# GpSimd subtracts a quarter of each weight piece of the second block, VectorE three quarters

## The chip, the cores and the metric

The kernel is written in Bass, engine by engine, with semaphores between the engines, and runs on one core of one Trainium2 chip. The metric is the device time of one execution in microseconds (us), the median of several runs. A profile of one execution is read with it. Its engines are PE (TensorE matmuls), PEld (its weight loads), DVE (VectorE), ACT (ScalarE), POOL (GpSimd) and SP (SyncE, which here issues the DMAs).

## The reference, cut to what matters

Two transformer stacks run one after the other on 256 tokens of width 1024. The first (`first_block`) has a hybrid mixer, an MLA mixer and two expert layers. The change is in the second, which has two equal layers:

```python
h = x
for i in range(DEPTH):                      # DEPTH = 2
    hn = rmsnorm_2(h, ln_mix[i])
    (aq, ak, av, hy, gq, gk, gv, go, glr, gates) = split_cols(hn @ w_in[i], IN_SPLITS)
    y_a = attention_mixer(aq, ak, av, attn_qnorm[i], attn_knorm[i], cos, sin) @ w_br_attn[i]
    y_b = hyena_mixer(hy, hy_conv[i], spec, hy_skip[i]) @ w_br_hyena[i]
    y_c = gla_mixer(gq, gk, gv, go, glr, gla_w_lr[i], gla_b_lr[i], gla_onorm[i]) @ w_br_gla[i]
    mixed = gate[:, :, 0] * y_a + gate[:, :, 1] * y_b + gate[:, :, 2] * y_c
    h = h + mixed @ w_out[i]
    h = h + memory_cross_attention(rmsnorm_2(h, ln_x[i]), rmsnorm_2(mem, ln_mem[i]), ...)
    hn = rmsnorm_2(h, ln_mlp[i])
    h = h + jnp.square(jax.nn.relu(hn @ mlp_w1[i])) @ mlp_w2[i]
```

All of it is float32. Every `@` with a weight matrix is such a product as the change touches.

## The kernel before, in words

**Products in three passes.** A float32 product is made of float32r products, whose operands keep fewer bits. Each weight piece `w` is split into a high part (ACT copies it to float32r) and a low part (`w` minus the high part, float32r again), and so is each activation. PE then adds up high x high, high x low and low x high (L374, L375, L376 in `split_steps`; L434 to L436 where tokens are the output rows; L404 and L406 in `paired_steps`, the last product of the MLP, with the first two passes in one matmul of 512 columns; L2020 to L2022 in `three_passes`).

**Pieces.** Weights come by DMA into the three slots of a ring in `big`, 4096 columns each. A slot is two pieces of 2048 columns (8 chunks of 256, 4 of 512 or 16 of 128). The high part goes to one of two places, `hot_split` and `high_split` in turn; the low part is written over the weights themselves (`ring_split` is `big` by another name). For piece p:

- ACT, `split_high` (L465): waits for the DMA and until PE is done with piece p-2, whose place it takes, copies, and raises `w_high`.
- DVE, `split_low` (L473): waits for `w_high`, subtracts, and raises `w_split`.
- PE, `next_piece` (L331): waits for `w_split` before the piece's first matmul.

So while PE works on piece p-1, ACT and DVE must make both parts of piece p. The second block has 174 pieces, 87 in each layer. All of its work stands in an order written out by hand: `split_high()` and `split_low()` calls stand between the other ACT and DVE work of a stage (evictions, norms, softmax, the convolution taps L3059 and L3061, the spectra L3086 to L3101, the gated sums L3209 and L3212), and each engine takes its instructions in that order. Before a product is ready to begin, the split activations have to be there too (L481 on ACT, L486 and L622 on DVE).

**GpSimd** works only in the two expert layers of the first block, where it subtracts for half of the expert weights (L2426, 1024 columns each). In the second block it has nothing to do.

Of the kernel before, what the change touches and what calls it, by code (L numbers as in the profile page):

```python
# [140 lines left out]
def two_blocks(nc, a, upto=99):  # L141
    ctx = ExitStack()
    with ctx:
# [183 lines left out]

        def next_piece(i, part):
            p = len(pieces)
            pieces.append((i, part))  # L330
            TE.wait_ge(S["w_split"], p + 1)  # L331
            w_low = piece(p, ring_r)
            return p, high_part(p, w_low), w_low
# [133 lines left out]
        def split_low():  # L467

            p = split_at["low"]
            split_at["low"] += 1  # L470
            VE.wait_ge(S["w_high"], p + 1)
            w = piece(p, big)
            VE.tensor_tensor(piece(p, ring_r), w, high_part(p, w).bitcast(F32), ALU.subtract)\  # L473
                .then_inc(S["w_split"], 1)

# [720 lines left out]
        def hybrid_pe():  # L1196
# [31 lines left out]
            frees(b, "gate_rows")  # L1228
# [14 lines left out]
            for lhs, rhs, name in ((z.k, z.k, "kk_out"), (z.k, z.q, "kq_out")):  # L1243
# [41 lines left out]
            for m_ in range(TM):  # L1285
                b = acquire("act")
                for g in range(GH):
                    for rows in halves:
                        i = mm(ps[rows, b, g * P:(g + 1) * P], z.inv[rows, 4 * m_ + g, :], z.vb[rows, m_, g, :],
                               start=True, stop=True)  # L1290
                i.then_inc(S["tile_for_act"], 1)
                frees(b, "uw_out")
            w_at = [acquire("act") for _ in halves]
            for n, m_, g in blocks:
                for b, rows in zip(w_at, halves):
                    i = mm(ps[:, b, n * GC:(n + 1) * GC], z.kbeg[rows, m_, g, :], z.inv[rows, n, :],
                           start=True, stop=True)
                    if n == len(blocks) - 1:
                        i.then_inc(S["tile_for_act"], 1)
                        frees(b, "uw_out")  # L1300
            for _ in run:
                pass
            TE.wait_ge(S["uw_out"], expected["uw_out"])
# [68 lines left out]
        def hybrid_act():  # L1372
# [95 lines left out]
            evict_act([g4(z.u, 0), g4(z.u, 1)], frees="uw_out", n=2)  # L1468
            evict_act([z.wT[:, :, GC * w:GC * w + GC] for w in range(2)], frees="uw_out", n=2)
# [24 lines left out]
        def hybrid_dve():  # L1494
# [69 lines left out]
            VE.tensor_tensor(split8(z.decT), t, lastdim(gcv[:, :, 0:4], GC), ALU.subtract).then_inc(S["gate_rows"], 1)  # L1564
            VE.wait_ge(S["gate_rows"], S.nth(VE, "gate_rows"))
# [41 lines left out]
            VE.tensor_tensor(z.qk, tile8(), z.decT, ALU.mult).then_inc(S["kq_out"], 1)  # L1607
            VE.wait_ge(S["kq_out"], S.nth(VE, "kq_out"))
# [18 lines left out]
            VE.wait_ge(S["uw_out"], S.nth(VE, "uw_out", 4))  # L1627
# [1099 lines left out]
        def mixer_linears(L):  # L2727
# [8 lines left out]
            yield from split_tm_steps("gla_v", x_high, x_low, 512, "act", "gla_v_in")  # L2736
# [14 lines left out]
        def mixers_pe(L):  # L2751
# [55 lines left out]
            for o in range(2):  # L2807
                TE.wait_ge(S["conv_in"], S.nth(TE, "conv_in"))
                for t in range(TM):
                    b = acquire("act")  # L2810
                    for c in range(4):
                        m = TE.transpose(ps[:, b, c * P:(c + 1) * P], z.u0[:, c, t * P:(t + 1) * P], C["ident"])
                    m.then_inc(S["tile_for_act"], 1)
                    frees(b, "time_major")
                turned = expected["time_major"]
# [3 lines left out]
                TE.wait_ge(S["time_major"], turned)  # L2819
# [49 lines left out]
            TE.wait_ge(S["gla_v_in"], expected["gla_v_in"])  # L2869
# [49 lines left out]
        def mixers_act(L):  # L2919
# [22 lines left out]
            def between(i):  # L2942
                if i < 2:
                    evict_act(pad[4 + i:5 + i], frees="hyena_in")
                elif i < 4:
                    evict_act([z.gq[:, 2 * i - 4:2 * i - 2, :]], frees="gla_qk_in")
                elif i < 6:
                    evict_act([z.gv[:, :, (i - 4) * T:(i - 3) * T]], frees="gla_v_in")
# [12 lines left out]
            for o in range(2):  # L2961
                if o == 1:
                    evict_act([z.gates[0][:, 4:6, :]], ACT.Sigmoid, frees="gate_in")
                evict_act([z.ut[:, t, :] for t in range(TM)], frees="time_major", n=2)
# [546 lines left out]
        def layer_pe(L):  # L3511
            filter_pe(L)
            mixers_pe(L)
# [164 lines left out]
```

## Time and profile before

| | us |
|---|---|
| median of 3 runs | 3422.14 (3418.97 to 3427.79) |
| the profiled execution, its own time | 3427.8 |
| its span, first to last instruction | 3426.0 |
| of it the second block, about 2126 to the end | 1300.0 |
| PE busy, whole span | 3295.8 |
| DVE, ACT, POOL busy, whole span | 2106.3, 1764.6, 636.9 |

The profiled execution is 5.7 us longer than the median of the runs. Its granted TensorE clock is 0.98 of full speed in the second block. A row of the timeline reads: start in us from the span's start, duration in us, engine, line of the kernel, operation, names written<-read with shapes, number of instructions merged into the row, and in brackets the idle time of the engine before it and what ended that.

### The profile page before, as it was taken

The page shows a single profiled execution, that of the slowest core. Times are in us where ns is not written, and L with a number is a line of the kernel's source. Part 1 is how long each engine was busy: PE and PEld are TensorE (multiplying, and loading weights), DVE is VectorE, ACT ScalarE, POOL GpSimd, SP SyncE. Part 2 cuts the span into 40 slices and gives each one's busy share as a digit, 9 for nine tenths or more (in the row PEclk, how much of TensorE's full clock was granted, in tenths as well). Part 3 has the DMA queues.
Part 4 walks back from the last instruction along what each step waited for, and adds up shares of the span by engine and source line. Part 5 has one row for each costly group of instructions (what it writes and reads, how often), then busy time and mean ns, then how long its engine had stood idle before and what let it go on. Part 6 is the DMA issues. An engine that isn't in the chain of part 4 may idle for free.

```text
span 3426.0 us, 56030 instructions
## 1 busy us (share of the span) xinstructions
PE 3295.8 (96%) x23252; PEld 3045.5 (89%) x23252; DVE 2106.3 (61%) x3187; ACT 1764.6 (52%) x2689; POOL 636.9 (19%) x260
## 2 busy tenths in 40 slices
PE   6889999999999989999999999999999999999999
PEld 6779999998888879999998887989999979899998
DVE  7654956657777556946655656475655456755544
ACT  4424556664454545566655554455455445555562
POOL 0000886660000004976630000000000000000000
PEclk8879999999999999999999999999999999999999
DMA  7443554448887434554456664423434633244355
GB/s 255 136 135 117 167 179 141 141 148 276 279 277 258 147 119 148 179 160 142 140 187 194 198 191 161 148 102 112 172 137 171 182 113 128 87 173 172 120 176 135
DMA packets 263983, 565.82 MB, mean 165 GB/s; under 512 B 15470, under 2 KB 94002, under 8 KB 262962
## 3 DMA queue, kind: packets, MB, share of 16 engines
q1 hardware_dynamic: 263732, 562.25, 50.3%
q8 instruction: 185, 3.03, 0.4%
q14 instruction: 66, 0.54, 0.1%
HBM read 561.16 MB, written 1.05 MB: 164 GB/s over the span
## 4 chain that ended last, share of the span: by engine, by line
PE 86%; DVE 6%; ACT 3%; DMA 2%; POOL 2%; issue 1%; SPq 0%; DVEq 0%; ACTq 0%
PE ps L374 8%; PE ps L376 8%; PE ps L375 8%; PE ps L2020 8%; PE ps L2021 7%; PE ps L2022 7%; PE ps L2103 7%; PE ps L2105 7%; PE ps L2104 7%; PE ps L2069 3%; PE ps L404 3%; POOL uvr_split L2426 2%; PE ps L406 2%; DVE ring_split L473 1%; PE ps L569 1%
## 5 line engine op out<-in xcount | busy, mean ns | idle before, releaser
L2426 POOL TENSOR_TENSOR uvr_split<-uvr,high_split 128x1024 fp32r<-128x1024 f32 x172 | 432.4, 2517 | 1038.9 <-ACT high_split L2150 1038.9
L2022 PE MATMUL ps<-consts_sb_split,uvr_split 128*128 128x256 f32 x2048 | 579.1, 283 | 0.0
L2150 ACT ACTIVATE high_split<-uvr 128x1024 fp32r<-128x1024 f32 x342 | 360.9, 1056 | 232.1 <-PE ps L2105 179.9
L376 PE MATMUL ps<-uvr_split,ring_split 128*128 128x256 f32 x1680 | 479.8, 286 | 0.0
L2021 PE MATMUL ps<-ht_split,high_split 128*128 128x256 f32 x1488 | 423.8, 285 | 0.0
L2020 PE MATMUL ps<-consts_sb_split,high_split 128*128 128x256 f32 x1392 | 403.0, 290 | 6.7 <-DVE ht_split L605 3.8
L473 DVE TENSOR_TENSOR ring_split<-big,high_split 128x2048 fp32r<-128x2048 f32 x111 | 251.8, 2268 | 253.8 <-ACT high_split L465 252.9
L473 DVE TENSOR_TENSOR ring_split<-big,hot_split 128x2048 fp32r<-128x2048 f32 (+2 forms) x111 | 248.7, 2240 | 255.5 <-ACT hot_split L465 254.8
L2104 PE MATMUL ps<-uvr_split,hot_split 128*128 128x512 f32 x1024 | 398.4, 389 | 0.0
L2022 PEld LDWEIGHTS ps<-consts_sb_split,uvr_split 128*128 128x128 f32 x2048 | 392.0, 191 | 0.0
L376 PEld LDWEIGHTS ps<-uvr_split,ring_split 128*128 128x128 f32 x1680 | 326.5, 194 | 0.0
L516 ACT ACTIVATE big<-ps 128x512 f32<-128x512 f32 (+2 forms) x225 | 130.3, 579 | 374.2 <-PE ps L376 242.1
L2021 PEld LDWEIGHTS ps<-ht_split,high_split 128*128 128x128 f32 x1488 | 288.7, 194 | 0.0
L375 PE MATMUL ps<-ht_split,high_split 128*128 128x256 f32 (+1 forms) x1000 | 286.0, 286 | 0.0
L465 ACT ACTIVATE high_split<-big 128x2048 fp32r<-128x2048 f32 x111 | 210.3, 1895 | 140.7 <-PE ps L376 69.9
L375 PE MATMUL ps<-ht_split,hot_split 128*128 128x256 f32 x992 | 282.3, 285 | 0.0
L2337 DVE TENSOR_TENSOR uvr_split<-uvr,high_split 128x1024 fp32r<-128x1024 f32 x170 | 208.2, 1225 | 119.5 <-ACT high_split L2150 117.9
L465 ACT ACTIVATE hot_split<-big 128x2048 fp32r<-128x2048 f32 (+2 forms) x111 | 207.8, 1872 | 141.0 <-PE ps L376 70.2
L2020 PEld LDWEIGHTS ps<-consts_sb_split,high_split 128*128 128x128 f32 x1392 | 267.2, 192 | 9.3 <-issue 4.2
L2103 PE MATMUL ps<-high_split,hot_split 128*128 128x512 f32 x680 | 265.6, 391 | 1.2 <-DVE hot_split L2340 1.2
L2105 PE MATMUL ps<-high_split,hot_split 128*128 128x512 f32 x680 | 264.7, 389 | 0.0
L374 PE MATMUL ps<-uvr_split,high_split 128*128 128x256 f32 (+1 forms) x840 | 245.0, 292 | 5.6 <-DVE ring_split L473 5.6
(470 smaller groups left out, 8392.9 us busy)
## 6 DMA issues: line engine op xcount, KB each, us to landing
uvr<-peer_uv SPq DMA_DIRECT2D x512, 512.0 KB, 3.9
big<-mlp_w SPq DMA_DIRECT2D x32, 2048.0 KB
big<-w_in SPq DMA_DIRECT2D x26, 2048.0 KB
uvr<-mod_w SPq DMA_DIRECT2D x56, 512.0 KB, 6.5
big<-peer_w_q SPq DMA_DIRECT2D x8, 2048.0 KB
big<-hy_w_in SPq DMA_DIRECT2D x6, 2048.0 KB
big<-mod_w SPq DMA_DIRECT2D x24, 512.0 KB, 3.9
big<-mod_w SPq DMA_DIRECT2D x8, 1024.0 KB
```

Source lines behind the costliest of these rows:

```text
L374: mm(out, wh, x_high[:, k, :], start=st, stop=False)
L375: mm(out, wh, x_low[:, k, :], start=False, stop=False)
L376: m = mm(out, wl, x_high[:, k, :], start=False, stop=en)
L465: SE.activation(high_part(p, w), w, ACT.Copy).then_inc(S["w_high"], 1)
L473: VE.tensor_tensor(piece(p, ring_r), w, high_part(p, w).bitcast(F32), ALU.subtract)\
L2020: mm(out, w_high, x_high, start=start, stop=False, **kw)
L2021: mm(out, w_high, x_low, start=False, stop=False, **kw)
L2022: return mm(out, w_low, x_high, start=False, stop=stop, **kw)
L2103: mm(out, p_high[:, tok], expert_high(e)[:, f], start=False, stop=False, skip_group_check=True)
L2104: mm(out, p_high[:, tok], expert_low(e)[:, f], start=False, stop=False, skip_group_check=True)
L2105: m = mm(out, p_low[:, tok], expert_high(e)[:, f], start=False, stop=False, skip_group_check=True)
L2426: GE.tensor_tensor(expert_low(j), expert(j), expert_high(j).bitcast(F32), ALU.subtract)\
```

## The change

The subtraction of a piece in the second block is shared between two engines. DVE takes the first three quarters of the piece's chunks of rows, GpSimd the last quarter. GpSimd's part waits for the same `w_high` as DVE's and raises a semaphore of its own, `w_split_rest`; PE waits for both before the piece's first matmul. The split of the first block's pieces stays as it was. To have a semaphore free, some existing ones are made to serve two purposes (`gate_rows` becomes `gate_sums`, `kq_out` `kk_out`, `uw_out` `delta_out`, `gla_v_in` `gla_qk_in`, `time_major` `probs_turned`).

```diff
+        shared = {}
+        sharing = [False]
+
+        def own_chunks(p, w):
+            return w.shape[1] - w.shape[1] // 4 if p in shared else w.shape[1]
+
         def next_piece(i, part):
             p = len(pieces)
             pieces.append((i, part))
             TE.wait_ge(S["w_split"], p + 1)
+            if sharing[0] and piece(p, big).shape[1] >= 4:
+                shared[p] = len(shared) + 1
+                TE.wait_ge(S["w_split_rest"], shared[p])
             w_low = piece(p, ring_r)
             return p, high_part(p, w_low), w_low
...
             w = piece(p, big)
-            VE.tensor_tensor(piece(p, ring_r), w, high_part(p, w).bitcast(F32), ALU.subtract)\
+            k = slice(0, own_chunks(p, w))
+            VE.tensor_tensor(piece(p, ring_r)[:, k, :], w[:, k, :], high_part(p, w)[:, k, :].bitcast(F32), ALU.subtract)\
                 .then_inc(S["w_split"], 1)
+
+        def split_rest_pool():
+
+            for p in shared:
+                GE.wait_ge(S["w_high"], p + 1)
+                w = piece(p, big)
+                k = slice(own_chunks(p, w), w.shape[1])
+                GE.tensor_tensor(piece(p, ring_r)[:, k, :], w[:, k, :], high_part(p, w)[:, k, :].bitcast(F32),
+                    ALU.subtract).then_inc(S["w_split_rest"], 1)
...
-            TE.wait_ge(S["gla_v_in"], expected["gla_v_in"])
+            TE.wait_ge(S["gla_qk_in"], expected["gla_qk_in"])
...
         def layer_pe(L):
             filter_pe(L)
+            sharing[0] = True
             mixers_pe(L)
...
                 peer_pool(1)
+            split_rest_pool()
```

On DVE, in the mixers of the second block's first layer, this stands in a row before (names: `ring_split` is a piece's low part, `w_high` the semaphore of ACT's copy; the lines after it are the convolution taps and the spectrum's first steps):

```order
L473 TENSOR_TENSOR ring_split<-big,high_split 128x8x256 [waits w_high,probs_ready]
L3051 COPY big<-ps 128x256 [waits tile_for_dve]
L473 TENSOR_TENSOR ring_split<-big,hot_split 128x8x256 [waits w_high,o_out]
L3059 TENSOR_SCALAR uvr<-big,vecs_sb 128x256 [waits hyena_in]
L3059 TENSOR_SCALAR uvr<-big,vecs_sb 128x256 x7
L3061 SCALAR_TENSOR_TENSOR uvr<-big,vecs_sb,uvr 128x256 [waits dve_step]
L3061 SCALAR_TENSOR_TENSOR uvr<-big,vecs_sb,uvr 128x256 x7
L3061 SCALAR_TENSOR_TENSOR uvr<-big,vecs_sb,uvr 128x256 [waits dve_step]
L3061 SCALAR_TENSOR_TENSOR uvr<-big,vecs_sb,uvr 128x256 x7
L473 TENSOR_TENSOR ring_split<-big,high_split 128x8x256 [waits w_high,dve_step]
```

and this after the change (L483 is what L473 was, L3078 and L3080 are the taps):

```order
L483 TENSOR_TENSOR ring_split<-big,high_split 128x6x256 [waits w_high,probs_ready]
L3070 COPY big<-ps 128x256 [waits tile_for_dve]
L483 TENSOR_TENSOR ring_split<-big,hot_split 128x6x256 [waits w_high,o_out]
L3078 TENSOR_SCALAR uvr<-big,vecs_sb 128x256 [waits hyena_in]
L3078 TENSOR_SCALAR uvr<-big,vecs_sb 128x256 x7
L3080 SCALAR_TENSOR_TENSOR uvr<-big,vecs_sb,uvr 128x256 [waits dve_step]
L3080 SCALAR_TENSOR_TENSOR uvr<-big,vecs_sb,uvr 128x256 x7
L3080 SCALAR_TENSOR_TENSOR uvr<-big,vecs_sb,uvr 128x256 [waits dve_step]
L3080 SCALAR_TENSOR_TENSOR uvr<-big,vecs_sb,uvr 128x256 x7
L483 TENSOR_TENSOR ring_split<-big,high_split 128x6x256 [waits w_high,dve_step]
```

The order on DVE is the same; each subtraction has 6 chunks of 256 columns instead of 8.

On POOL, after the last expert subtraction (where its program ended before), these rows follow in the changed kernel, 174 in all:

```order
L2445 TENSOR_TENSOR uvr_split<-uvr,high_split 128x1024 [waits expert_high] x2
L492 TENSOR_TENSOR ring_split<-big,hot_split 128x2x256 [waits w_high]
L492 TENSOR_TENSOR ring_split<-big,high_split 128x2x256 [waits w_high]
L492 TENSOR_TENSOR ring_split<-big,hot_split 128x512 [waits w_high]
L492 TENSOR_TENSOR ring_split<-big,high_split 128x256 [waits w_high]
L492 TENSOR_TENSOR ring_split<-big,hot_split 128x2x256 [waits w_high]
```

Each waits for nothing but the high part of its piece, so POOL has no other work between two of them.

## Rows read from the trace of the kernel before

**Rows 1.** The second block's first layer: span, busy us (count) of PE, PEld, DVE, ACT, POOL; clock; DMA

```profile
2126.00:2778.00 652.00, 635.66 (x4619) 586.77 (x4618) 374.76 (x442) 326.79 (x370) 0.00 (x0) 0.98 0.43 143
```

**Rows 2.** Waits of PE in the second block: us in total, times, longest us

```profile
PE ps L374 <- DVE ring_split L473: 9.6, 8, 2.7
...
PE ps L2835 <- DVE big L3097: 5.4, 2, 2.7
```

**Rows 3.** Timeline, an MLP piece: ACT, DVE and PE's first matmul; the last piece's DVE, PE

```profile
2617.08 1.92 ACT L465 ACTIVATE high_split<-big 128x2048 fp32r<-128x2048 f32 x1 [2.04 <-PE ps L376]
2619.03 2.29 DVE L473 TENSOR_TENSOR ring_split<-big,high_split 128x2048 fp32r<-128x2048 f32 x1 [2.87 <-ACT high_split L465]
2622.56 0.28 PE L374 MATMUL ps<-uvr_split,high_split 128*128 128x256 f32 x1
3410.57 2.29 DVE L473 TENSOR_TENSOR ring_split<-big,high_split 128x2048 fp32r<-128x2048 f32 x1 [2.64 <-ACT high_split L465]
3413.95 0.40 PE L404 MATMUL ps<-rest_split,high_split 128*128 128x512 f32 x1
```

**Rows 4.** Groups of DVE instructions: busy us, mean ns of one | idle before

```profile
L2337 DVE TENSOR_TENSOR uvr_split<-uvr,high_split 128x1024 fp32r<-128x1024 f32 x170 | 208.2, 1225 | 119.5 <-ACT high_split L2150 117.9
L486 DVE TENSOR_TENSOR ht_split<-ht,uvr_split 128x512 fp32r<-128x512 f32 x28 | 18.1, 687 | 0.2
```

**Rows 5.** Timeline, first block's expert layer: POOL and DVE where they meet

```profile
361.58 2.29 DVE L2254 TENSOR_TENSOR big<-big 128x2048 f32<-128x2048 f32 x1
361.59 4.54 POOL L2426 TENSOR_TENSOR uvr_split<-uvr,high_split 128x1024 fp32r<-128x1024 f32 x1 [0.48 <-ACT high_split L2150]
391.68 2.40 POOL L2426 TENSOR_TENSOR uvr_split<-uvr,uvr_split 128x1024 fp32r<-128x1024 f32 x1
391.75 4.46 DVE L2271 TENSOR_TENSOR big<-big 128x2048 f32<-128x2048 f32 x1
```

**Rows 6.** Timeline: ACT's copy and the POOL subtraction that waits for it

```profile
1499.94 1.05 ACT L2150 ACTIVATE high_split<-uvr 128x1024 fp32r<-128x1024 f32 x1
1501.07 2.40 POOL L2426 TENSOR_TENSOR uvr_split<-uvr,high_split 128x1024 fp32r<-128x1024 f32 x1 [1.36 <-ACT high_split L2150]
```

**Rows 7.** Timeline, place A: DVE and PE's first matmul of the piece

```profile
2171.73 2.29 DVE L473 TENSOR_TENSOR ring_split<-big,hot_split 128x2048 fp32r<-128x2048 f32 x1 [6.79 <-ACT hot_split L465]
2174.07 0.58 PE L374 MATMUL ps<-uvr_split,hot_split 128*128 128x256 f32 x1 [1.05 <-DVE ring_split L473]
```

**Rows 8.** Timeline, place B: DVE's chain to the spectrum, ACT's second copy, PE's wait

```profile
2268.42 2.29 DVE L473 TENSOR_TENSOR ring_split<-big,hot_split 128x2048 fp32r<-128x2048 f32 x1 [0.74 <-ACT hot_split L465]
2272.85 6.55 DVE L3061 SCALAR_TENSOR_TENSOR uvr<-big,vecs_sb,uvr 128x256 f32<-128x256 f32 x16
2275.42 1.91 ACT L465 ACTIVATE high_split<-big 128x2048 fp32r<-128x2048 f32 x1
2289.97 0.76 PE L2835 MATMUL ps<-uvr,big 128*128 128x256 f32 x1 [2.68 <-DVE big L3097]
```

**Rows 9.** Timeline, place C: ACT's copy, DVE, PE's first matmul of the piece

```profile
2381.61 1.91 ACT L465 ACTIVATE high_split<-big 128x2048 fp32r<-128x2048 f32 x1 [2.61 <-issue]
2384.07 1.29 DVE L486 TENSOR_TENSOR rest_split<-big,rest_split 128x512 fp32r<-128x512 f32 x2 [2.84 <-ACT rest_split L481]
2387.62 0.39 PE L374 MATMUL ps<-uvr_split,high_split 128*128 128x256 f32 x1 [2.73 <-DVE ring_split L473]
```

**Rows 10.** Timeline, place D: ACT's copy and DVE one piece earlier, PE's wait

```profile
2434.90 1.92 ACT L465 ACTIVATE hot_split<-big 128x2048 fp32r<-128x2048 f32 x1 [3.74 <-PE ps L376]
2436.92 2.29 DVE L473 TENSOR_TENSOR ring_split<-big,hot_split 128x2048 fp32r<-128x2048 f32 x1 [0.58 <-ACT hot_split L465]
2447.69 0.38 PE L2020 MATMUL ps<-rest_split,high_split 128*128 128x256 f32 x1 [1.39 <-DVE ring_split L473]
```

**Rows 11.** Timeline, place E: a piece with little to spare, DVE and PE

```profile
2158.93 2.29 DVE L473 TENSOR_TENSOR ring_split<-big,hot_split 128x2048 fp32r<-128x2048 f32 x1 [9.34 <-ACT hot_split L465]
2161.79 0.28 PE L374 MATMUL ps<-uvr_split,hot_split 128*128 128x256 f32 x1
```

More of the change, by code:

```diff
@@ L1227, in hybrid_pe @@
             mm(ps[:, b, :], C["blk"], z.N, start=True, stop=True).then_inc(S["tile_for_dve"], 1)
-            frees(b, "gate_rows")
+            frees(b, "gate_sums")
             rows_at = [acquire("act") for _ in halves]
@@ L1242, in hybrid_pe @@
                     frees(b, name)
-            for lhs, rhs, name in ((z.k, z.k, "kk_out"), (z.k, z.q, "kq_out")):
+            for lhs, rhs, name in ((z.k, z.k, "kk_out"), (z.k, z.q, "kk_out")):
                 b = acquire("dve")
@@ L1291, in hybrid_pe @@
                 i.then_inc(S["tile_for_act"], 1)
-                frees(b, "uw_out")
+                frees(b, "delta_out")
             w_at = [acquire("act") for _ in halves]
@@ L1299, in hybrid_pe @@
                         i.then_inc(S["tile_for_act"], 1)
-                        frees(b, "uw_out")
+                        frees(b, "delta_out")
             for _ in run:
                 pass
-            TE.wait_ge(S["uw_out"], expected["uw_out"])
+            TE.wait_ge(S["delta_out"], expected["delta_out"])
             TE.wait_ge(S["att_in"], expected["att_in"])
@@ L1467, in hybrid_act @@
                     logs_and_exps()
-            evict_act([g4(z.u, 0), g4(z.u, 1)], frees="uw_out", n=2)
-            evict_act([z.wT[:, :, GC * w:GC * w + GC] for w in range(2)], frees="uw_out", n=2)
+            evict_act([g4(z.u, 0), g4(z.u, 1)], frees="delta_out", n=2)
+            evict_act([z.wT[:, :, GC * w:GC * w + GC] for w in range(2)], frees="delta_out", n=2)
             evict_act([moba[5]], frees="att_in")
@@ L1563, in hybrid_dve @@
             t = take("dve").rearrange("p (m g n) -> p m g n", m=TM, g=GH)
-            VE.tensor_tensor(split8(z.decT), t, lastdim(gcv[:, :, 0:4], GC), ALU.subtract).then_inc(S["gate_rows"], 1)
-            VE.wait_ge(S["gate_rows"], S.nth(VE, "gate_rows"))
+            VE.tensor_tensor(split8(z.decT), t, lastdim(gcv[:, :, 0:4], GC), ALU.subtract).then_inc(S["gate_sums"], 1)
+            VE.wait_ge(S["gate_sums"], S.nth(VE, "gate_sums"))
             VE.scalar_tensor_tensor(out=z.dec, in0=z.decT, scalar=-1.0, in1=half8(C["mlow"]), op0=ALU.mult,
@@ L1606, in hybrid_dve @@
                 VE.wait_ge(S["dve_step"], S.nth(VE, "dve_step"))
-            VE.tensor_tensor(z.qk, tile8(), z.decT, ALU.mult).then_inc(S["kq_out"], 1)
-            VE.wait_ge(S["kq_out"], S.nth(VE, "kq_out"))
+            VE.tensor_tensor(z.qk, tile8(), z.decT, ALU.mult).then_inc(S["kk_out"], 1)
+            VE.wait_ge(S["kk_out"], S.nth(VE, "kk_out"))
             split_low()
@@ L1626, in hybrid_dve @@
             rotate_dve(z.ak, 4, z.cos, z.sin, z.tmp, "k_rotated")
-            VE.wait_ge(S["uw_out"], S.nth(VE, "uw_out", 4))
+            VE.wait_ge(S["delta_out"], S.nth(VE, "delta_out", 4))
             VE.tensor_scalar(small[:, 2:3], small[:, 0:1], 1.0, None, ALU.mult).then_inc(S["state_ready"], 1)
@@ L2735, in mixer_linears @@
             yield from split_steps("gla_qk", x_high, x_low, DC, 512, "act", "gla_qk_in")
-            yield from split_tm_steps("gla_v", x_high, x_low, 512, "act", "gla_v_in")
+            yield from split_tm_steps("gla_v", x_high, x_low, 512, "act", "gla_qk_in")
             yield from split_steps("gla_o", x_high, x_low, DC, 512, "act", "projections")
@@ L2813, in mixers_pe @@
                     m.then_inc(S["tile_for_act"], 1)
-                    frees(b, "time_major")
-                turned = expected["time_major"]
+                    frees(b, "probs_turned")
+                turned = expected["probs_turned"]
                 if o == 0:
@@ L2818, in mixers_pe @@
                     logits()
-                TE.wait_ge(S["time_major"], turned)
+                TE.wait_ge(S["probs_turned"], turned)
                 for part in range(2):
@@ L2947, in between @@
                 elif i < 6:
-                    evict_act([z.gv[:, :, (i - 4) * T:(i - 3) * T]], frees="gla_v_in")
+                    evict_act([z.gv[:, :, (i - 4) * T:(i - 3) * T]], frees="gla_qk_in")
                 elif i < 8:
@@ L2963, in mixers_act @@
                     evict_act([z.gates[0][:, 4:6, :]], ACT.Sigmoid, frees="gate_in")
-                evict_act([z.ut[:, t, :] for t in range(TM)], frees="time_major", n=2)
+                evict_act([z.ut[:, t, :] for t in range(TM)], frees="probs_turned", n=2)
                 if o == 0:
```

## The prediction, on record before the changed kernel ran

> **What bounds the kernel now.** Read the stretches of the second block first, since nothing of the first block's work changes. In its first layer PE is busy 635.7 of 652 us [rows 1]: the block is bound by matmuls, and all that the change can give or take lies in the idle time of PE, about 16 us there, or in idle time that it makes. Then read who PE waits for. Eight waits at the first matmul of a piece, 9.6 us together, end with DVE's subtraction L473, and two, 5.4 us, with the spectrum L3097, which stands on DVE behind two subtractions [rows 2]. Third, read how much time an ordinary piece has to spare. In the MLP DVE ends the low part at 2619.03 + 2.29 = 2621.32 and PE begins the piece at 2622.56: 1.24 us. For the very last piece it is 3413.95 - 3412.86 = 1.09 [rows 3]. Some forty pieces of each layer have 1.0 to 1.3 us, and most others, in the mixers, more than 2.
>
> **The parts of the change, each by itself.** DVE's part goes from 2048 to 1536 columns. 1024 columns take 1.225 us [rows 4] and 2048 take 2.29 [rows 3]; halfway is 1.76. It saves 0.53 us.
>
> GpSimd's part has 512 columns. The trace has only 1024, in 2.40 us [rows 5]. Half of that, 1.20, is the lower bound; the upper one, no gain from the smaller size, is 2.40. On DVE 512 columns take 0.687 of 1.225 us, a share of 0.56 [rows 4]; the same share of 2.40 is 1.35, which I take, because a fixed part of each instruction is likelier than none or all of it.
>
> If the two ran side by side, the piece would be ready 0.53 us sooner. They don't, by the trace. At 361.58 DVE begins a TENSOR_TENSOR with both inputs in SBUF, POOL begins its own at 361.59, and that one takes 4.54 us instead of 2.40: it ends 2.26 us after DVE's, as if begun then. At 391.75 it is the other way: POOL is at work since 391.68, and DVE's instruction takes 4.46 instead of 2.29, ending 2.13 us after POOL's [rows 5]. So one waits for the whole of the other, and some 0.15 us of start-up is saved at the change-over. There are twelve such stretched POOL instructions in the trace, each beside a DVE TENSOR_TENSOR with both inputs in SBUF. L473 is just that form, and the new POOL part is the other one.
>
> Both wait for the same `w_high`. POOL starts 0.08 us after ACT's end [rows 6]; DVE starts 0.03 after it in the MLP [rows 3] and 0.10 after it where the instruction also waits for something else [rows 10]. So who comes first changes, but the sum hardly does. DVE first: 0.03 + 1.76 + 1.35 - 0.14 = 3.00 us from ACT's end to both parts done, before 0.03 + 2.29 = 2.32, so +0.68. POOL first: 0.08 + 1.35 + 1.76 - 0.16 = 3.03, before 0.10 + 2.29 = 2.39, so +0.64. I take **+0.65 us for each piece whose ACT copy ends last**. With 1.20 for POOL it is +0.50, with 2.40 it is +1.70.
>
> The extra wait on PE costs nothing by itself: it stands at the same matmul as the old one, and pieces there already carry two or three waits while MLP pieces follow each other without idle time. The shared semaphores keep their order on each engine; I count them as nothing, with the evictions that they tell of over long before the waits.
>
> **Where +0.65 reaches PE.** An ordinary piece has 1.09 to 1.24 us to spare, of which 0.05 is the handover itself [rows 3, 7]: it stays hidden, with 0.4 us left. What counts are these places, once in each layer:
>
> - A: the piece at 2174.07 waits for DVE already, which waited for ACT [rows 7]: +0.65.
> - B: the spectrum. DVE's chain runs from the subtraction at 2268.42 through the taps to PE's wait at 2289.97. The first subtraction has POOL before it: +0.65. The second piece's copy ends at 2277.33, in the middle of the L3061 instructions, which also read two tensors of SBUF [rows 8]. If POOL cuts in there, they wait 1.2 us and the next subtraction gives back 0.53: +0.65. Together +1.3.
> - C: at 2387.62. POOL would start at 2383.60 and hold up the two L486 at 2384.07 until about 2384.9, +0.8, then -0.53 from the subtraction [rows 9]: +0.3. The piece before it, at 2378.88, waits for DVE as well, but its +0.65 goes into PE's 2.73 us of waiting here.
> - D: at 2447.69. ACT's copy of this piece stands behind DVE's gated sums, and those behind the subtraction at 2436.92 [rows 10]: +0.65 there, and +0.65 for the piece itself, so +1.3.
> - E: five pieces have 0.49 to 0.69 us to spare, such as 2161.79 - 2161.22 = 0.57 [rows 11]. With 0.05 for the handover, 0.65 exceeds that by 0.14 here, by 0.6 over the five.
> - The eighth kind of wait, at 2205.85, has DVE late with its own work for 5 us; POOL holds that work up by at most 1.2 us and the subtraction gives 0.53 back: nothing, between -0.5 and +0.7.
>
> The sum is 0.65 + 1.3 + 0.3 + 1.3 + 0.6 = 4.15 us a layer, **8.3 us** in both. By the lower bound for POOL it is some 5 us. The profiled execution, 3427.8 us with a span of 3426.0, would come to 3436.1; it lies 5.7 us above the median of the runs, so from the median the forecast is 3422.1 + 8.3 = 3430.4 us.
>
> The part of place B that rests on L3061 isn't shown by any row: no SCALAR_TENSOR_TENSOR meets POOL in this trace. [...]
>
> **The rivals.**
>
> 1. Side by side. POOL's part would be hidden beside DVE's, and the subtraction 0.53 shorter wherever it ends last: A, C, the two of B and of D, and 2205.85 give 7 x 0.53 = 3.7 us a layer, 7.4 in both: 3414.7. For it: POOL is idle in the whole block [rows 1]. Against it: rows 5, without exception.
>
> 2. Slower by far more, through DVE's chains in the mixers. Every copy that ends while DVE is at two-input work lets POOL cut into it for 1.2 us. Softmax weights, rotations, gated sums and state updates that PE takes from DVE then come later by 0.65 net or more, where I count only B and D. It decides where such a result has under 0.65 us to spare. If of some 40 mixer and attention pieces of a layer each fourth passed on half a microsecond, it would be +5 a layer, +18 in all: 3440. For it: PE's waits are few now, and waits that don't show may be near. Against it: pieces in the mixers have over 2 us to spare on their own path.
>
> 3. POOL's part is hardly shorter than 1024 columns. From 1.75 us on, a piece comes more than 1.05 later and the MLP's cover is gone. At 2.40 each of some 44 steady pieces a layer would cost (1.70 - 1.05) / 2 = 0.33 (two pieces are under way at a time), +29 in both, and the places above 2.6 times their price, +22: about 3473.
>
> 4. The sharing doesn't take place. The order of the changed program speaks against it: 174 POOL rows, DVE with 6 of 8 chunks.
>
> **How the numbers follow.** About 0.3%, 10.3 us, is what a measurement of this kernel can tell from no change. The forecast (serial, +4 to +14) has 0.60, of which I put 0.45 within 0.3% and 0.15 above. Rival 1 has 0.09, 0.07 within and 0.02 faster. Rival 2 has 0.25, nearly all slower, rival 3 0.05, rival 4 0.01. That makes faster 0.02, same 0.54, slower 0.44. The range leaves out rival 3, the upper end of rival 2 and the lower end of rival 1: 3417 to 3444.
>
> **What would show it.** In the changed profile: L483 at 1.76 us where it is alone and about 3.1 where POOL has begun before it; POOL's L492 at about 1.35 alone and near 3.0 where it waits for DVE; both parts ready 3.0 us after ACT's copy; in the MLP no idle time of PE and some 0.4 us left; PE's waits at A, D and L2835 longer by 0.65, 1.3 and 1.3. The prediction would be wrong if L483 stayed at 1.76 everywhere (rival 1), if waits of PE for L748 or other DVE lines appeared in the mixers (rival 2), or if L492 alone took over 1.75 us (rival 3).

## The result, and the profile after

The changed kernel takes 3436.73 us, the median of 5 runs (3435.23 to 3441.57), against 3423.53 of the kernel before, also 5 runs (3418.97 to 3427.79): a ratio of 1.0038, 95% interval 1.0027 to 1.0050. It was measured a second time (the last experiment): 3434.56 against 3423.34, ratio 1.0037 (1.0025 to 1.0050). So the change makes the kernel slower by 11 to 13 us. The forecast was 3430.4, 8.3 us slower, range 3417 to 3444. The two profiled executions take 3435.2 and 3427.8 us and are 7.4 us apart.

The page and two rows of windows, which answer to [rows 1] (the columns are as there; the second row is the second layer):

```profile
span 3433.4 us, 56238 instructions
...
PE 3293.6 (96%) x23252; PEld 3042.7 (89%) x23252; DVE 2142.5 (62%) x3187; ACT 1764.2 (51%) x2689; POOL 986.9 (29%) x434
...
2126.00:2778.00 652.00, 633.03 (x4607) 583.89 (x4606) 392.64 (x441) 324.45 (x366) 174.90 (x87) 0.98 0.43 143
2778.00:3433.00 655.00, 631.65 (x4612) 584.56 (x4610) 387.24 (x428) 323.43 (x367) 175.05 (x87) 0.98 0.42 137
```

POOL has 174 instructions more, 350 us. DVE was to get less work, 0.53 us for each of 170 full pieces, and shows 36 us more than before (2142.5 against 2106.3): that is the first thing to see, since it can only be time in which its instructions stand still. The groups of the two new parts, those with `high_split` (busy us, then the mean ns of one):

```profile
L492 POOL TENSOR_TENSOR ring_split<-big,high_split 128x512 fp32r<-128x512 f32 x85 | 173.1, 2036 | 471.5 <-ACT high_split L474 471.4
L483 DVE TENSOR_TENSOR ring_split<-big,high_split 128x1536 fp32r<-128x1536 f32 x85 | 190.6, 2243 | 203.2 <-ACT high_split L474 202.8
```

A mean of 2.24 us for 1536 columns, where 2048 took 2.29. The mean mixes two cases, which the timeline shows apart. First a piece of the MLP, as in [rows 3]: ACT, DVE and POOL (start, duration, engine):

```profile
2618.45 1.92 ACT L474 ACTIVATE high_split<-big 128x2048 fp32r<-128x2048 f32 x1 [2.04 <-PE ps L385]
2620.40 1.76 DVE L483 TENSOR_TENSOR ring_split<-big,high_split 128x1536 fp32r<-128x1536 f32 x1 [2.30 <-ACT high_split L474]
2620.44 2.87 POOL L492 TENSOR_TENSOR ring_split<-big,high_split 128x512 fp32r<-128x512 f32 x1 [2.89 <-ACT high_split L474]
2622.21 1.65 DVE L3521 TENSOR_TENSOR rest_split<-uvr,rest_split 128x512 fp32r<-128x512 f32 x1
2623.93 0.28 PE L383 MATMUL ps<-uvr_split,high_split 128*128 128x256 f32 x1
```

DVE comes first and takes 1.76 us; POOL, 0.04 later, ends at 2623.31, 1.15 us after DVE. Its 2.87 us are 1.3 of work behind some 1.6 of standing still. DVE's next instruction, L3521, which is L3502 of before (684 ns there), then stands behind POOL for about 1 us. Both parts are ready 2.94 us after ACT's copy ends at 2620.37, before it was 2.32; the piece has 0.62 us left before PE needs it. At place D it is the other way round:

```profile
2435.46 1.30 POOL L492 TENSOR_TENSOR ring_split<-big,hot_split 128x512 fp32r<-128x512 f32 x1 [4.66 <-ACT hot_split L474]
...
2435.49 2.89 DVE L483 TENSOR_TENSOR ring_split<-big,hot_split 128x1536 fp32r<-128x1536 f32 x1 [0.29 <-ACT hot_split L474]
...
2444.54 2.84 POOL L492 TENSOR_TENSOR ring_split<-big,high_split 128x512 fp32r<-128x512 f32 x1 [7.78 <-ACT high_split L474]
...
2447.48 0.56 PE L2039 MATMUL ps<-rest_split,high_split 128*128 128x256 f32 x1 [2.61 <-issue]
2447.83 0.42 PE L2040 MATMUL ps<-rest_split,high_split 128*128 128x256 f32 x1
2448.05 0.41 PE L2041 MATMUL ps<-rest_split,ring_split 128*128 128x256 f32 x1
```

POOL is first by 0.03 us, takes 1.30, and DVE's 1.76 become 2.89: ready 2.99 us after the copy, before 2.39. So whoever starts second waits for the whole of the other, and the sum hardly depends on the order. At 2447.48 PE has waited 2.61 us, before 1.39 [rows 10]. "issue" stands where the wait ended with POOL's part. From the second matmul behind this wait on, they start 0.21 us apart and no longer 0.12: the clock, told below.

PE's waits in the second block, which answer to [rows 2] (us in total, times, longest):

```profile
PE ps L383 <- DVE ring_split L483: 7.4, 8, 1.9
...
PE ps L2854 <- DVE big L3116: 6.4, 2, 3.2
PE ps L2039 <- issue: 5.2, 2, 2.6
...
PE ps L383 <- issue: 3.8, 4, 1.9
```

**Where the time went, place by place.** The start of PE's first matmul of each of the 174 pieces was taken from both traces. A growth that comes at the second matmul of a late piece counts with it. After minus before is -2.37 us at the first piece of the second block (in the first block nothing changed: that is scatter) and +7.37 at the last: the second block is 9.74 us longer in this pair. Where that difference grows from one piece to the next, a piece became late:

| place | forecast, a layer | layer 1 | layer 2 |
|---|---|---|---|
| A, 2174.07 | +0.65 | +0.42 | +0.59 |
| B, piece 2267.40 and spectrum | +1.3 | +1.10 | +1.09 |
| C, with 2378.88 before it | +0.3 | -0.20 | +0.19 |
| D, 2447.69 | +1.3 | +1.23 | +1.25 |
| E, pieces with 0.49 to 0.69 to spare | +0.6 | +0.91 | +0.9 |
| 2205.85 | 0 | -0.28 | -0.27 |
| branch pieces, 2417.68 to 2434.64 | 0 | +0.63 | +0.66 |
| smaller ones | 0 | +0.0 | +0.1 |
| sum of waits | +4.15 | +3.80 | +4.48 |
| stretches at a lower clock | 0 | -0.01 | +1.47 |

The waits make 8.28 us, the clock 1.46 net. (The times name the pieces by their place in the trace of before; those of the second layer come some 650 us later. B is +0.57 at the piece and +0.53 at the spectrum, C -0.79 behind +0.59 at 2378.88.)

**Branch pieces.** This place was in no step of the prediction. DVE around 2426.7 in the changed kernel, and in the kernel before at the same place in the program:

```profile
2423.86 2.88 DVE L483 TENSOR_TENSOR ring_split<-big,hot_split 128x1536 fp32r<-128x1536 f32 x1 [0.31 <-ACT hot_split L474]
2426.66 0.68 DVE L3228 TENSOR_TENSOR big<-ps,big 128x512 f32<-128x512 f32 x1
```

```profile
2425.62 2.29 DVE L473 TENSOR_TENSOR ring_split<-big,hot_split 128x2048 fp32r<-128x2048 f32 x1 [0.58 <-ACT hot_split L465]
2427.83 0.68 DVE L3209 TENSOR_TENSOR big<-ps,big 128x512 f32<-128x512 f32 x1
```

The gated sum L3228 empties a bank of `ps`, and comes 2.80 us behind the start of the subtraction, before 2.21. PE's piece that begins at 2427.49 has had both its weight parts for 0.75 us by then:

```profile
2427.14 0.28 PE L385 MATMUL ps<-rest_split,ring_split 128*128 128x256 f32 x1
2427.49 0.36 PE L383 MATMUL ps<-rest_split,hot_split 128*128 128x256 f32 x1
2427.68 0.28 PE L384 MATMUL ps<-rest_split,hot_split 128*128 128x256 f32 x1
```

PE begins it 0.15 us after the gated sum's end at 2427.34, and 0.35 us behind the matmul before it, where 0.12 is usual. The wait is one for a free bank: PE fills four banks in turn for DVE, the one it needs next is the one that this gated sum has just read, and `acquire` (L235) waits for `branch_in`, which L3228 raises. In the trace that wait ends at 2427.43 and L3228's signal comes at 2427.35, while POOL's part was done at 2425.13 and DVE's at 2426.74. The second matmul follows 0.19 us behind the first where 0.12 is usual: where a wait is new, it costs 0.07 to 0.10 us more than the first matmul's lateness.

**Place B.** The taps L3080 (L3061 before), SCALAR_TENSOR_TENSOR with two inputs in SBUF, take 542 ns in the mean of 32, before 480: 2.0 us in all, 1.0 a layer. In each layer a single one is stretched, to 1.50 us: POOL's part has begun before it.

```profile
L3080 DVE SCALAR_TENSOR_TENSOR uvr<-big,vecs_sb,uvr 128x256 f32<-128x256 f32 x32 | 15.1, 542 | 0.1
```

**The clock.** The same stretch behind a wait, in windows of the trace: at A of before, of the changed kernel, and of its second measurement, and at D of before and of the changed kernel. The granted clock is the third number from the end, behind POOL's.

```profile
2174.00:2180.00 6.00, 5.92 (x37) 5.93 (x38) 2.31 (x2) 2.97 (x3) 0.00 (x0) 0.72 1.03 383
```

```profile
2171.00:2177.00 6.00, 5.71 (x27) 5.74 (x28) 1.76 (x1) 2.76 (x3) 3.04 (x2) 0.50 1.03 379
2447.00:2455.00 8.00, 7.52 (x53) 7.55 (x54) 2.07 (x2) 0.69 (x2) 3.23 (x2) 0.79 0.63 240
```

```profile
2169.50:2180.00 10.50, 10.20 (x75) 9.91 (x76) 3.29 (x2) 6.80 (x8) 4.56 (x3) 1.00 0.60 220
```

```profile
2447.00:2454.00 7.00, 6.31 (x53) 6.31 (x54) 3.28 (x3) 2.18 (x2) 0.00 (x0) 1.00 0.88 300
```

At D of the changed kernel the clock is 0.50 from 2446.98 to 2450.39, 3.4 us, and the matmuls start 0.21 us apart; from 2450.40 to 2455 it is 1.00, and they start 0.12 us apart. Behind D the lower clock cost 1.25 and 1.47 us in the two layers, behind A 1.22 more than before (first layer), while a stretch behind C that before has (0.79 from 2387 to 2395) is gone, -1.47, and another at the block's start cost 1.01 less. The same kernel in its second profile has a clock of 1.00 behind A. So these stretches aren't tied to the change alone.

### The profile page after: what moved, and what is told of

It reads as the page before. It is cut to its first block, busy times and chain, and to the rows that moved or that the text cites. A ratio compares the mean times of both kernels' runs of the same rounds, so it can differ in the third digit from the quotient of the medians.

```text
span 3433.4 us, 56238 instructions
## 1 busy us (share of the span) xinstructions
PE 3293.6 (96%) x23252; PEld 3042.7 (89%) x23252; DVE 2142.5 (62%) x3187; ACT 1764.2 (51%) x2689; POOL 986.9 (29%) x434
## 4 chain that ended last, share of the span: by engine, by line
PE 85%; DVE 6%; DMA 3%; ACT 3%; POOL 2%; issue 1%; SPq 0%; DVEq 0%; ACTq 0%
PE ps L383 8%; PE ps L385 8%; PE ps L384 8%; PE ps L2039 8%; PE ps L2040 7%; PE ps L2041 7%; PE ps L2122 6%; PE ps L2124 6%; PE ps L2123 6%; PE ps L2088 3%; PE ps L413 3%; POOL uvr_split L2445 2%; PE ps L415 2%; DVE ring_split L483 1%; PE ps L588 1%
## 5 line engine op out<-in xcount | busy, mean ns | idle before, releaser
L492 POOL TENSOR_TENSOR ring_split<-big,hot_split 128x512 fp32r<-128x512 f32 (+1 forms) x87 | 174.9, 2010 | 836.7 <-ACT hot_split L474 836.6
L483 DVE TENSOR_TENSOR ring_split<-big,high_split 128x1536 fp32r<-128x1536 f32 (+1 forms) x111 | 247.3, 2228 | 243.1 <-ACT high_split L474 242.4
L483 DVE TENSOR_TENSOR ring_split<-big,hot_split 128x1536 fp32r<-128x1536 f32 (+3 forms) x111 | 244.2, 2200 | 246.2 <-ACT hot_split L474 245.5
L492 POOL TENSOR_TENSOR ring_split<-big,high_split 128x512 fp32r<-128x512 f32 x87 | 175.1, 2012 | 480.0 <-ACT high_split L474 479.9
L2122 PE MATMUL ps<-high_split,hot_split 128*128 128x512 f32 x680 | 265.7, 391 | 2.6 <-DVE hot_split L2359 2.6
```

What stands on the lines that cost most here:

```text
L483: VE.tensor_tensor(piece(p, ring_r)[:, k, :], w[:, k, :], high_part(p, w)[:, k, :].bitcast(F32), ALU.subtract)\
L492: GE.tensor_tensor(piece(p, ring_r)[:, k, :], w[:, k, :], high_part(p, w)[:, k, :].bitcast(F32), ALU.subtract).then_inc(S["w_split_rest"], 1)
L2122: mm(out, p_high[:, tok], expert_high(e)[:, f], start=False, stop=False, skip_group_check=True)
```

## The experiments

Each stands against runs of the kernel before that were taken beside it (median 3423.85 for the first four, 3424.00 for the next four). Piece times are read as above, experiment minus before. Where a diff starts from the changed kernel, it shows only what differs from that.

**The sharing left out, the names kept.**

```diff
-            sharing[0] = True
```

> The changed kernel with the sharing switched off: the semaphores still serve two purposes, GpSimd has no part. Theory (serial subtractions at a few places, plus half-clock stretches of TensorE after longer waits): the names cost nothing, 0 +- 3 us against the kernel before. Rival (the shared semaphores or a longer wait list delay PE): it keeps a good part of the +13 us.

Measured: 3424.03 us against 3423.85, ratio 1.0001 (0.9992 to 1.0010), 11 and 19 runs. Through the whole second block its piece times run in parallel to those of before, at +6.1 to +6.4 us, all of it from the first block. The shared semaphores cost nothing; the same profile shows that two executions of the same work may differ by 6 us.

**DVE's three quarters alone.** POOL's part and PE's wait for it are gone. The low parts' last quarter isn't computed; so that nothing depends on it, PE takes the high part in the low part's place in the second block, with the same shapes.

```diff
-                TE.wait_ge(S["w_split_rest"], shared[p])
...
-            return p, high_part(p, w_low), w_low
+            return p, high_part(p, w_low), high_part(p, w_low) if p in shared else w_low
...
-            split_rest_pool()
```

> The changed kernel without GpSimd's part and without PE's wait for it; the last quarter of each low part is left out, and PE's low pass in the second block reads the high part again (same number and size of matmuls). Theory: VectorE's part takes 1.76 us everywhere and wherever it ends last PE starts 0.53 sooner: seven times a layer, 5 to 8 us faster than before, some 18 us faster than the changed kernel. Rival (PE's or VectorE's side of the new order is what costs, not GpSimd): no gain against before.

Measured: 3413.77 us, ratio 0.9971 (0.9961 to 0.9981), 9 runs.

```profile
L482 DVE TENSOR_TENSOR ring_split<-big,hot_split 128x1536 fp32r<-128x1536 f32 x85 | 149.5, 1758 | 233.3 <-ACT hot_split L473 233.0
...
PE ps L382 <- DVE ring_split L482: 6.1, 8, 2.5
PE ps L2853 <- DVE big L3115: 3.4, 2, 1.7
```

1536 columns are 1.758 us, the 1.76 of the prediction, in each of the 170. The gain of 10 us is what sharing would have brought if POOL's part disturbed nothing; the prediction's first rival put it at 7.4. The places that gain are those it names, 0.45 at A, 0.54 at 2205.85 and at 2378.88, 1.08 at D, and one that it doesn't: 0.68 at 2767.06, at the end of the first layer's MLP.

**POOL at work at the same time, but only writing.** POOL waits for the same semaphore and raises the same one, PE waits for it, but the instruction is a memset of the same 512 columns. Here too PE takes the high part for the low one.

```diff
-                GE.tensor_tensor(piece(p, ring_r)[:, k, :], w[:, k, :], high_part(p, w)[:, k, :].bitcast(F32),
-                    ALU.subtract).then_inc(S["w_split_rest"], 1)
+                GE.memset(w[:, k, :], 0.0).then_inc(S["w_split_rest"], 1)
```

> As the one before it, but GpSimd keeps its instruction, its wait for w_high and its semaphore, and PE waits for it: only it fills the quarter with zeros (writes, reads nothing of SBUF) instead of subtracting. Theory (the two subtractions exclude each other because both read two tensors of SBUF): VectorE stays at 1.76 us, and the time is that of the kernel without GpSimd's part within 2 us. Rival (any GpSimd instruction at that moment delays VectorE, or its semaphore comes late): L483 is stretched again and the time is near the changed kernel's.

Measured: 3411.85 us, ratio 0.9966 (0.9952 to 0.9979), 5 runs, no slower than without POOL.

```profile
L492 POOL MEMSET big<- 128x512 f32 x170 | 89.5, 526 | 1530.6 <-ACT hot_split L474 944.2 <-ACT high_split L474 586.4
...
L483 DVE TENSOR_TENSOR ring_split<-big,high_split 128x1536 fp32r<-128x1536 f32 x85 | 149.4, 1758 | 238.2 <-ACT high_split L474 237.7 <-DVE big L779 0.3
...
PE ps L383 <- DVE ring_split L483: 5.2, 8, 1.5
```

The second semaphore, the second wait on PE and an instruction on POOL cost nothing together. DVE's part stays at 1758 ns although a memset begins beside nearly every one, and its own mean of 526 ns shows no standing still either. So neither POOL's presence nor its writing costs; what the subtraction does and the memset doesn't is to read SBUF. A memset is also shorter than the subtraction, 0.53 against 1.29 us, so this run can't say what a writing instruction of 1.3 us would do. No experiment changed DVE's side. For that the kernel before has a pair in its first block: a DVE TENSOR_TENSOR with one input in `ps` (PSUM) and one in SBUF overlaps a POOL subtraction for 2.24 us, and neither is stretched, where the same pair with both inputs in SBUF was [rows 5].

```profile
382.29 2.41 POOL L2426 TENSOR_TENSOR uvr_split<-uvr,uvr_split 128x1024 fp32r<-128x1024 f32 x1 [0.48 <-ACT uvr_split L2150]
382.46 2.29 DVE L2268 TENSOR_TENSOR big<-ps,big 128x2048 f32<-128x2048 f32 x1
```

DVE's part with `high_split` takes 1758 ns in the mean beside the memset and 2243 in the changed kernel, beside the subtraction.

**Half of each piece for POOL.**

```diff
-            return w.shape[1] - w.shape[1] // 4 if p in shared else w.shape[1]
+            return w.shape[1] - w.shape[1] // 2 if p in shared else w.shape[1]
```

> GpSimd subtracts half of each piece's chunks instead of a quarter. Theory: 1.22 + 2.40 - 0.14 us in a row, a piece is ready about 1.2 us later than before instead of 0.6, so the places that wait cost twice as much: +17 to +25 us in the second block against before, and the MLP, with 1.02 to 1.19 us to spare, just begins to wait. Rival (a fixed price per piece, of the semaphore or the wait): the same +10 to +13 as with a quarter.

Measured: 3462.76 us, ratio 1.0116 (1.0101 to 1.0132), 4 runs. This is +39 us, and the second block of the profile is 33 us longer; the expectation of +17 to +25 there was too low.

```profile
L492 POOL TENSOR_TENSOR ring_split<-big,high_split 128x1024 fp32r<-128x1024 f32 x84 | 243.7, 2901 | 416.4 <-ACT high_split L474 416.4
L483 DVE TENSOR_TENSOR ring_split<-big,high_split 128x1024 fp32r<-128x1024 f32 x84 | 180.3, 2146 | 203.9 <-ACT high_split L474 203.4
...
PE ps L2039 <- issue: 7.2, 2, 3.6
```

In the MLP POOL's part now takes 3.44 us, since it waits for DVE's of 1.23; both parts come about 1.2 us later than before the change, and the cover of 1.09 to 1.24 us is used up: nearly every piece there is 0.05 to 0.19 us late, where in the changed kernel one or two are. D costs 2.29 and 2.30, the branch pieces up to 0.55 each, B and the piece ahead of it 2.2. What was mis-sized is the places with little cover, for which the expectation took twice their former price. Once the cover is gone they pay in full: 0.77 at 2161.79, which cost 0.18, and 3.8 us in the first layer's MLP, which cost 0.3. Some waits are new, such as 0.62 at 2203.88. A fixed price of each shared piece is excluded, since as many pieces are shared as before and the cost is three times as high.

**All pieces shared but two at D in each layer.**

```diff
-            if sharing[0] and piece(p, big).shape[1] >= 4:
+            ours = p - (first_shared[0] or 0)
+            if sharing[0] and piece(p, big).shape[1] >= 4 and ours % 87 not in (36, 37):
```

> The changed kernel, with VectorE doing the whole of two pieces of each layer: those of place D (the piece whose subtraction stood at 2436.92 before, and the one that PE begins at 2447.69). Theory (a wait there of 2.61 us instead of 1.39, and behind it 3.4 us of TensorE at half clock): both go, PE's wait is 1.4 us again, no half-clock stretch follows it, and 2.5 us a layer come back, 5 of the changed kernel's 9.7 in the second block: 3430 to 3433. Rival (the half clock has another cause than this wait): the wait goes back, the half-clock stretch stays, and 2.5 us come back.

Measured: 3434.14 us, ratio 1.0029 (1.0017 to 1.0041), 6 runs.

```profile
2446.73 0.39 PE L2041 MATMUL ps<-rest_split,high_split 128*128 128x256 f32 x1 [1.36 <-DVE ring_split L485]
```

D's wait is back at 1.36 us (1.39 before the change, 2.61 with it), the difference of the piece times grows there by -0.02 in both layers, and the clock behind it stays at 1.00. So D's share of the sum, 2.5 us in both layers, is shown in the trace. The median is 10.1 us above before, where the changed kernel had 13.2 and 11.2, and just outside the 3430 to 3433 expected; the medians alone don't resolve 2.5 us.

**Only those two pieces in each layer shared**, 4 of 174: the condition of the last diff with `in` for `not in`.

> The complement: only those two pieces of each layer are shared, four of 174. Theory: PE's wait of 2.6 us and the half-clock stretch behind it are there, +2.5 us a layer, +5 in all, while the rest of the second block keeps the times of before. Rival (half clock only with the load of all the shared pieces): +1.2 us a layer and no half clock.

Measured: 3427.82 us, ratio 1.0017 (1.0008 to 1.0026), 11 runs.

```profile
2446.54 0.36 PE L2041 MATMUL ps<-rest_split,high_split 128*128 128x256 f32 x1 [2.61 <-issue]
2446.73 0.28 PE L2042 MATMUL ps<-rest_split,high_split 128*128 128x256 f32 x1
...
2446.00:2454.00 8.00, 7.46 (x64) 7.49 (x65) 2.98 (x2) 2.02 (x2) 0.44 (x1) 1.00 0.65 246
```

The wait is the same 2.61 us as in the changed kernel, and the growth is +1.23 in both layers: D's price is a matter of its own two pieces. The median is 3.8 us above before, 1.3 more than these two growths. But the matmuls behind it start 0.12 us apart and the clock is 1.00, in both layers. My theory that the longer wait brings the lower clock with it fell here: that part needs something more than the wait at D.

**Only the MLP's pieces shared**, 64 of 174:

```diff
-            sharing[0] = True
             mixers_pe(L)
             cross_pe(L)
+            sharing[0] = True
             mlp_pe(L)
+            sharing[0] = False
```

> Only the MLP's pieces are shared, 64 of 174. Theory: each is ready 0.6 us later, and nearly all of it lies in the 1.1 to 1.2 us that they have to spare: PE's first matmuls in the MLP stand 0.3 us later per layer, 0 to +1 us in all. Rival (a price for each shared piece): 64/174 of the loss, +4 to +5 us.

Measured: 3424.72 us against 3424.00, ratio 1.0006 (0.9997 to 1.0015), 11 and 23 runs. In the MLP the piece times move only at its second piece, which had 0.49 us to spare (+0.22, and +0.07 at its second matmul), and at 2767.06 (+0.05); in the second layer at the second piece again, +0.29. Outside it they move by up to 0.15 us and by one stretch at a lower clock. Where an MLP piece has 1.09 us or more to spare, 0.6 us later costs nothing, as the prediction had it. About 0.6 of the loss is in the MLP, the rest in mixers and attention.

**The other way: no second engine, but an earlier start.** This is the kernel before; POOL does nothing in the second block. DVE subtracts each piece in two halves of its chunks, in both blocks, and PE waits for the first half at the piece's first matmul and for the second ahead of the first matmul that reads it.

```diff
-            TE.wait_ge(S["w_split"], p + 1)
+            TE.wait_ge(S["w_split"], 2 * p + 1)
...
+        def second_half(p, kk):
+            if p not in rest_awaited and kk >= piece(p, big).shape[1] // 2:
+                rest_awaited.add(p)
+                TE.wait_ge(S["w_split"], 2 * p + 2)
...
+            half = w.shape[1] // 2
+            for k in (slice(0, half), slice(half, w.shape[1])):
+                VE.tensor_tensor(piece(p, ring_r)[:, k, :], w[:, k, :], high_part(p, w)[:, k, :].bitcast(F32),
+                    ALU.subtract).then_inc(S["w_split"], 1)
```

> The kernel before without GpSimd, but VectorE subtracts each piece in two instructions of half its chunks, and PE may begin the piece after the first: it waits for the second half ahead of the first matmul that reads it. Theory (what counts is only how soon PE can begin the pieces at a few places): the first half is ready 1.07 us sooner (1.22 instead of 2.29), the second 0.15 later but under cover, so A, 2205.85, C, the piece at 2267.40 and D give 0.5 to 1.1 each: 8 to 12 us faster than before, less if VectorE's chain at B, 0.3 us longer a layer, takes some of it. Rival (the pieces' latency isn't what costs): no change or slower by VectorE's extra 0.15 us a piece.

Measured: 3413.28 us (3407.55 to 3413.71, 6 runs), ratio 0.9966 (0.9953 to 0.9978): 10.7 us faster than before, and by the two measurements of the changed kernel 21 to 23 us faster than that.

```profile
L486 DVE TENSOR_TENSOR ring_split<-big,hot_split 128x1024 fp32r<-128x1024 f32 x170 | 200.7, 1222 | 201.7 <-ACT hot_split L476 201.4
...
PE ps L383 <- DVE ring_split L486: 4.1, 3, 2.5
...
PE ps L2848 <- DVE big L3110: 5.8, 2, 2.9
...
PE ps L2033 <- DVE ring_split L486: 0.8, 2, 0.4
```

Two halves are 2.44 us of DVE for 2.29, but the first is there after 1.22. At A, 2205.85, 2378.88 and D PE begins sooner by 0.83 to 1.27 us each, 8.0 in both layers. The piece at 2267.40, which the expectation counted too, gives 0.07: it had no wait before. The first layer's 2767.06 gives 0.68; the rest of the 10.7 isn't placed. B, which waits for all of DVE's chain, gains nothing (2.9 for 2.7).

**The changed kernel once more**, for the size of the result and for the clock.

> The changed kernel once more, beside the kernel before. The profiles put 8.3 us of its loss on PE's longer waits and 1.5 on TensorE's half-clock stretches, 9.7 in the second block; the medians said 13.2, with an interval of 9 to 17. Theory (nothing else in it): the median comes out 8 to 13 us above before, and in the profile the waits of PE are those of the first profile, while the half-clock stretches of a few us may stand at other places. Rival (something costs outside the places found): 13 us or more again, with first matmuls of pieces late where the first profile has none late.

Measured: 3434.56 us against 3423.34 (6 and 10 runs), +11.2, within the +8 to +13 expected. In the profile the second block is 8.45 us longer than before (-3.85 at its first piece, +4.60 at its last).

```profile
PE ps L383 <- DVE ring_split L483: 7.3, 8, 2.0
...
PE ps L383 <- issue: 3.5, 2, 2.0
```

The waits are those of the first profile to 0.3 us, and the waits of the table recur within 0.1 us, except at C (-0.13 and +0.08). The stretches at a lower clock do not recur: none behind A, one behind C as before the change, both behind D as in the first profile (+1.47 and +1.48), and behind the second layer's spectrum the clock is 0.50 for 6.8 us, before the change for 3.4 (+1.25).

## Why the prediction was right, and where it wasn't

**The mechanism.** Right. The two parts exclude each other, and the piece comes 0.60 us later (2.32 to 2.94, 2.39 to 2.99), forecast 0.65. DVE's part was to take 1.76 and took 1.76. POOL's was to take 1.35 and took 1.29: of the two ends, 1.20 and 2.40, the value near half of 1024 columns' time was the right choice, and the remaining 0.06 is most of the difference between 0.60 and 0.65. That POOL's reading, and not the signalling or the names, does it is shown by the memset and by the names alone.

**The cover in the MLP.** Right: PE doesn't wait for any piece that had 1.09 us or more to spare, and 0.49 to 0.62 us are left, 0.4 forecast. The MLP alone costs nothing that the medians show.

**D and B.** Right in place and nearly in size, 1.24 for 1.3 and 1.10 for 1.3. Part of B rested on SCALAR_TENSOR_TENSOR waiting like TENSOR_TENSOR, which no row of before showed: the second +0.65 of B was the author's estimate, and no run shows it in that size. The changed kernel shows one tap of each layer stretched to 1.50 us, 542 ns in the mean of all for 480, and the spectrum 0.53 us later behind the 0.57 of the piece.

**A.** 0.42 and 0.59 for 0.65. The chain behind A's wait begins with a DMA (start, us): first layer before and after, then second layer before and after.

```profile
2161.98 7.72 DMA big<-w_in
2158.59 7.69 DMA big<-w_in
2813.76 7.98 DMA big<-w_in
2815.18 8.12 DMA big<-w_in
```

It brings the weights that ACT then copies, and was issued when the piece ahead of 2161.79 ended, which wasn't late. So the 0.18 of the piece at 2161.79 goes into A's wait, and the two places share one delay of 0.60 (0.18 + 0.42), where the sum counted both A and that piece of E. In the second layer the two come to 0.78, and 0.14 of it is the DMA, which took 8.12 us for 7.98.

**C.** Right in the mechanism, half in the size. The piece ahead, 2378.88, came 0.59 later as forecast and went into PE's wait here, 1.94 us where it was 2.73. DVE's two L486, L505 in the changed kernel, are held up by 0.68 (0.8 forecast), and the subtraction ends 0.14 us later from the copy's end (4.05 to 4.19), forecast 0.3. The copy itself hangs on a DMA issued before 2378.88 came late. Its last part lands 9.20 us after the issue before the change and 8.86 after it, in the second layer 7.70 and 7.74. With 0.14 and 0.15 from DVE that gives the -0.20 and +0.19 of the table. Why the first layer's DMA was 0.34 us quicker isn't known.

**2205.85.** Forecast nothing, between -0.5 and +0.7; it gained 0.28 and 0.27. DVE is late there with its own work, and begins the subtraction 0.26 us later behind ACT's copy (5.31 to 5.57), but that is 0.53 shorter.

**E.** Mis-sized: 0.9 for 0.6. Four places pay, 2161.79, 2400.72, 2507.16 and 2593.76. Their first matmuls come late by 0.09, 0.18, 0.09 and 0.23, together 0.59, as forecast. What the step left out comes at the matmul behind the first, another 0.07 to 0.10 at each, 0.34 together: at 2161.79 of the changed kernel it starts 0.23 us behind the first and not 0.12.

**The branch pieces.** The step that failed. "An ordinary piece stays hidden" looked only at the way from subtraction to PE. L483 is at 2.88 us there, DVE's gated sums behind it come 0.6 us later, and PE waits for the bank that they empty: +0.65 a layer, 1.3 in both, put at nothing. This is the second rival's mechanism, the longer way through DVE's other work, at one place and not at ten.

**The sum.** The waits come to 8.28 us, forecast 8.3. The agreement to 0.1 us is luck: terms that were too large (A, B, C, D and 2205.85, 2.0 us in both layers) stand against the branch pieces and E (1.9). What the sum left out altogether is the clock, +1.5 net in the first profile. The two profiles' second blocks, +9.7 and +8.5, lie near the forecast; the medians, +13.2 and +11.2, lie 3 to 5 us above it. Part of that is the clock too, by the mean granted clock of each run. The changed kernel's 11 runs have 0.9796 in the mean, 52 runs of the kernel before 0.9806, and among those 52 a clock lower by 0.001 goes with 2.2 us more. At the same clock of 0.980, 6 runs of the changed kernel take 3435.6 us in the mean and 13 of before 3424.7. By this estimate some 2 us of the loss are a lower clock and 11 are not; the 2 to 3 us between that and the waits remain unexplained. The first block alone differs by -2.4, +6 and -3.9 us between profiles of the same code, so single profiles can't place them. The prediction put its largest chance on a time within 0.3%, and the ratio came out at 1.0038 and 1.0037, just above it, with both intervals reaching down past it. The sum gave +0.24%.

## What to carry to other kernels

Before you give a share of a VectorE subtraction to GpSimd, look in the trace for a stretched pair of the two engines: if one such pair waits in full, two engines are a queue, and the sum of both parts (here 1.76 + 1.29 less 0.14 at the change-over) is what counts against the whole on one engine (2.29). A wait that ends with such a subtraction is better shortened by releasing it in halves, which needs no other engine and gave 10.7 us here (in both blocks of the kernel). When a step delays an engine, follow what stands behind it in that engine's order too, not only its own result, since covers of 0.6 us and of 1.2 us look alike in a list of waits: neither shows in it. And ask what a waiting engine's chain hangs on: a DMA issued ahead of a delay isn't made later by it, so the delay goes into the wait (A and C here).

## What the runs showed of the hardware that was not expected

- A memset on POOL of 512 columns (0.53 us) beside DVE's subtraction with two inputs in SBUF holds up neither; a subtraction on POOL of 512 columns (1.29 us) holds DVE's up by 1.13 us (2.89 for 1.76), its whole length but for 0.16.
- The instruction that has to wait shows as a longer one and not as idle time: DVE's busy time rose by 36 us while its work fell by 0.53 us a piece. Only the groups' means, or two rows side by side in the timeline, tell.
- Each 3.4 us of PE at a granted clock of 0.50, with matmuls 0.21 us apart for 0.12, cost 1.0 to 1.5 us. The same 2.61 us wait had such a stretch behind it in four cases of four in the changed kernel and in none of two where only D's pieces are shared; behind A (a wait of 1.5 us) the same kernel had one in one execution and none in the other. What decides it was not found.
